# Byte distances between the matmuls' moving tiles and their weights: 64 everywhere, then 32, 48 and 80

## The chip, the cores and the metric

The kernel runs on one core of one Trainium2 chip. The metric is the device time of one execution in microseconds. Before the change it is 876.7 us, the median of 3 runs (870.92, 876.7 and 877.1 us).

## The reference

Two transformer blocks, one after the other, on 256 tokens of width 1024, all in float32. Cut to what matters:

```python
def first_block(x, p, ...):
    h = rms_norm(x, g_pre_mix); proj = h @ w_in                      # 1024 -> 1952
    o_sb = stick_breaking_attention(...); q = rms_norm(q_lat) @ w_q_up; kv = rms_norm(kv_lat) @ w_kv_up
    o_mla = mla_attention(...)
    x = x + rms_norm(concat(rms_norm(o_sb), rms_norm(o_mla)) @ w_o)
    u = causal_depthwise_conv(rms_norm(x) @ w_up)                     # 1024 -> 5632
    x = x + rms_norm((gelu(gate) * val) @ w_down)                     # 2816 -> 1024
    return x + rms_norm(sigmoid(rms_norm(x) @ w_ple_gate + b) * (p @ w_ple))

def hybrid_layer(x, mem, ...):                                        # the second block
    xn = rms_norm(x); proj = xn @ w_in                                # 1024 -> 5912
    # attention over compressed, selected and windowed keys; a 31-tap convolution; attention over mem
    merged = gates(xn) * (o_nsa @ w_nsa_out, u @ w_conv_out, o_m @ w_mem_out)
    h = x + merged @ w_out
    return h + (silu(rms_norm(h) @ w_gate) * (rms_norm(h) @ w_up)) @ w_down
```

Nearly all the work is products of a [256 x K] activation with a [K x M] weight matrix that is used once.

## The kernel before

**Weights.** All weight matrices come from memory as one stream of tiles of 128 x 1024 float32, eight blocks of 128 x 128 each. For each tile SyncE loads `raw` (a ring of 5), ScalarE rounds it into `whi` (fp32r, a ring of 6; line 1118), and VectorE or GpSimd takes the difference as `wlo` (lines 1636 and 609).

**Activations** are split the same way. Each chunk of 128 features is a row of 512 fp32r numbers in one tile: 256 high parts, then 256 low parts. `HA` holds the normed input of most stages, `ACTS` the products of both feed-forward networks, `HB` the normed memory and a few branch inputs, `HL` the latents and other small inputs.

**The product.** One 128 x 128 block of weights against one chunk takes three matmuls (`blk3`, called by `fm`), each with a weight load of its own and a moving operand of 256 columns:

```python
nc.tensor.matmul(dst, wh, hi, start=start, stop=False, skip_group_check=True)   # line 626
nc.tensor.matmul(dst, wl, hi, start=False, stop=False, skip_group_check=True)   # line 627
last = nc.tensor.matmul(dst, wh, lo, start=False, stop=stop, skip_group_check=True)   # line 628
```

In `tm` (lines 669 to 671) the roles are swapped: the activation chunk is loaded as weights, and `whi` or `wlo` moves with up to 512 columns. At lines 1010 to 1012 the loaded operand is `BS`, 30 columns (120 bytes) per step, and `whi` or `wlo` moves with 256 columns. Sums of squares (lines 683 and 688) and the attention's matmuls are plain float32.

**Addresses.** Tiles lie one behind the other in the order of their declarations, each from a multiple of 32 bytes on. The declarations around the change are

```python
SQ = sb("SQ", [P, DC, S])
sb("before_ha", [P, 112])
HA = sb("HA", [P, DC, 2 * S], F32R)
HB = sb("HB", [P, DC, 2 * S], F32R)
HL = sb("HL", [P, 4, 2 * S], F32R)
sb("behind_hl", [P, 144])
KMEM = sb("KMEM", [P, MEMH, S])
```

`raw`, `whi`, `wlo`, `X`, `Y` and `SQ` start at 0 modulo 128 bytes (in one partition). A chunk is 2048 bytes, its low half is 1024 bytes further, and a block of weights is 512 bytes, so every block and every half starts where its tile does, modulo 128. The two unused tiles move what lies behind them: 112 numbers are 448 bytes, or 64 modulo 128, and 112 + 144 = 256 numbers are 1024 bytes. The last declarations are regions that share one address, the end of everything else. Starts modulo 128, as the compiled program has them:

| tile | before | after |
|---|---|---|
| `raw`, `whi`, `wlo`, `X`, `Y`, `SQ` | 0 | 0 |
| `HA` | 64 | 32 |
| `HB` | 64 | 48 |
| `HL` | 64 | 80 |
| `KMEM`, `VMEM`, `RTT`, `RS`, `ident`, `ones`, `lower` | 0 | 96 |
| `ACTS`, `YC`, `G1`, `PX`, `QS`, `KS1`, `QM`, `KM`, `Z` | 64 | 32 |
| `BS`, step c of 16 | 64 + 120 c | 32 + 120 c |
| `VS2`, `QME`, `U`, `CY`, `PR2`, `OMEM` | 32 | 0 |

The order of all instructions on each engine is written out in the program and is not touched.

Of the kernel before, what the change touches and what calls it, by code (L numbers as in the profile page):

```python
# [9 lines left out]
F32R = mybir.dt.float32r  # L10
# [6 lines left out]
P = 128  # L17
S = 256
D = 1024
DC = D // P  # L20
# [280 lines left out]
def program(nc, stream, xT, memT, pT, pos, consts, w2, out):  # L301
    ctx = ExitStack()
    with ctx:
        def sb(name, shape, dt=F32):
            return ctx.enter_context(nc.sbuf_tensor(name, shape, dt))
# [9 lines left out]
        X = sb("X", [P, DC, S])  # L315
        Y = sb("Y", [P, DC, S])
        SQ = sb("SQ", [P, DC, S])
        sb("before_ha", [P, 112])
        HA = sb("HA", [P, DC, 2 * S], F32R)
        HB = sb("HB", [P, DC, 2 * S], F32R)  # L320
        HL = sb("HL", [P, 4, 2 * S], F32R)
        sb("behind_hl", [P, 144])
        KMEM = sb("KMEM", [P, MEMH, S])
        VMEM = sb("VMEM", [P, QT, 512])
        RTT = sb("RTT", [P, 2, 2 * S])
# [287 lines left out]
        def _(pe):  # L613
# [20 lines left out]
            def fm(stage, m, H, need=None, base=0):  # L634

                k = KC[stage]
                dst = begin((stage, m))[:, 0:S]
                for c in range(k):
                    if need is not None:
                        pe.wait_ge(a_lo, need + c + 1)  # L640
                    blk3(dst, FIRST[stage] + m * k + c, H[:, base + c, 0:S], H[:, base + c, S:2 * S],
                         c == 0, c == k - 1, c == k - 1)
# [35 lines left out]
            def stat(name, chunks, mat=ones, wide=False):  # L678

                dst = begin(("stat", name))  # L680
                if wide:
                    pe.wait_ge(sq_ready, SQ0[name] + dict(NORMS)[name])
                    nc.tensor.matmul(dst, mat[:, :], chunks, start=True, stop=True).then_inc(y_done, 1)
                    return
                for i in range(len(chunks)):
                    pe.wait_ge(sq_ready, SQ0[name] + i + 1)
                    w = 2 * CMP if name == "kc" else S
                    last = nc.tensor.matmul(dst[:, 0:w], mat[:, :], chunks[i][:, 0:w], start=i == 0,  # L688
                                            stop=i == len(chunks) - 1)
                last.then_inc(y_done, 1)  # L690
# [53 lines left out]
            def sb_pv(u):  # L744
                pe.wait_ge(sb_a, u + 1)
                o_begin(("sb", u))
                for j in range(2):
                    h = 2 * u + j
                    v = slice(h * DH, (h + 1) * DH)
                    o0 = OP[:, j * DH:(j + 1) * DH]  # L750
                    o1 = OP[:, P + j * DH:P + (j + 1) * DH]
                    nc.tensor.matmul(o0, Z[:, h, 0:P], VS1[:, 0, v], start=True, stop=True, skip_group_check=True)
                    nc.tensor.matmul(o1, Z[:, h, P:S], VS1[:, 0, v], start=True, stop=False, skip_group_check=True)
                    last = nc.tensor.matmul(o1, Z[:, h, S:384], VS1[:, 1, v], start=False, stop=True,
                                            skip_group_check=True)
                last.then_inc(o_ready, 1)
# [75 lines left out]
            def turn_out(use, src, ready, count):  # L832

                pe.wait_ge(ready, count)
                t_begin(use)
                for c in range(4):
                    for qt in range(QT):
                        last = nc.tensor.transpose(TP[:, c * S + qt * P:c * S + (qt + 1) * P],
                                                   src[:, qt, c * P:(c + 1) * P], ident[:, :])
                    if c == 1:  # L840
                        last.then_inc(t_half, 1)
                last.then_inc(t_ready, 1)
# [24 lines left out]
            for name, m in UPS:  # L867
                if name == "qup":
                    fm("qup", m, HL, SP0["ql"] if m == 0 else None)
                    if m == 0:  # L870
                        sb_cum(3)
                else:
                    if m == 1:
                        wait_freed(pe, ("sbv", 1))
                    if m:
                        sb_pv(m - 1)
                    fm("kup", m, HL, SP0["kvl"] if m == 0 else None, base=2)
            sb_pv(3)
# [16 lines left out]
            scores(("mla", 1))  # L895
            tm("vup", 512, HL, base=2)
            fm("memk", 0, HB, SP0["mem"])
            turn_out(("osb", 0), OSB, o_normed, 2)
# [20 lines left out]
            for m in range(1, 4):  # L919
                fm("memk", m, HB)  # L920

# [31 lines left out]
            for m in range(2):  # L953
                fm("ple", m, HL, SP0["p"] if m == 0 else None)
            stat("postffn", [SQ[:, c, :] for c in range(8)])
            for m in range(2, 8):
                fm("ple", m, HL)
            stat("plegate", [SQ[:, c, :] for c in range(8)])
# [3 lines left out]

            tm("memv", 512, HB, ks=range(0, 5))
            stat("mix2", [SQ[:, c, :] for c in range(8)])
            tm("memv", 512, HB, ks=range(5, 8))

# [54 lines left out]
            def fill(item, between=None):  # L1021
# [33 lines left out]
                if name in ("gnsb", "brnsa"):  # L1055
                    fm(name, m, HA if name == "gnsb" else HL, SP0["on"] if name == "brnsa" and m == 0 else None)
                    return
                H, base, split = {"brmem": (HB, 4, "om"), "brconv": (HB, 0, "cv")}[name]
                b = FIRST[name] + 12 * m
# [33 lines left out]
            for m in range(8):  # L1093
                fm("wout", m, HB, SP0["y"] if m == 0 else None)

# [1355 lines left out]
```

## Time and profile before

| | |
|---|---|
| median of 3 runs | 876.7 us |
| the profiled execution | 873.64 us |
| its span, first to last instruction | 871.9 us |
| TensorE busy | 826.1 us (95%), 6722 matmuls in the records |
| weight loads busy | 789.6 us (91%) |
| VectorE, ScalarE, GpSimd busy | 638.7, 498.8, 317.6 us |
| mean granted TensorE clock | 0.994 |

Matmuls overlap: the record of one lasts longer than the distance from its start to the next one's start. What a stream of matmuls costs is therefore read from the starts in the timeline (the last start less the first, divided by the intervals between them), and not from the mean duration. The other runs have times but no traces.

### The profile page before, as it was taken

How to read it: one execution, taken by the hardware profiler on the slowest of the kernel's cores; microseconds unless marked ns; L12 is line 12 of the kernel's file. 1: busy time of each engine (PE TensorE's matmuls, PEld its weight loads, DVE VectorE, ACT ScalarE, POOL GpSimd, SP SyncE). 2: the span in 40 equal slices, each digit the busy share in tenths (PEclk: the TensorE clock that was granted, in tenths of full speed). 3: DMA queues.
4: the chain of work that ended last, by engine and by line, in shares of the span. 5: the costliest groups of instructions: out<-in, count | busy, mean ns of one | idle time of the engine just before them, and what ended most of it. 6: DMA issues, size and time to landing. Idle time of an engine off the chain costs nothing.

```text
span 871.9 us, 16984 instructions
## 1 busy us (share of the span) xinstructions
PE 826.1 (95%) x6722; PEld 789.6 (91%) x6722; DVE 638.7 (73%) x981; ACT 498.8 (57%) x914; POOL 317.6 (36%) x148
## 2 busy tenths in 40 slices
PE   4999999999999999999999789899999999999998
PEld 3998889899999999788999779788999999999998
DVE  6895764888887772768799889955665676667774
ACT  6665655854665657756766474367546544444441
POOL 3843213122333225344466534332454223322321
PEclk9999999999999999999999999999999999999999
DMA  5743234355766665352656542322464457666651
GB/s 209 269 157 107 73 98 145 99 181 152 242 222 188 199 192 170 111 172 98 202 171 192 178 137 74 96 73 77 142 190 149 146 171 230 183 193 191 194 170 49
DMA packets 57246, 137.18 MB, mean 157 GB/s; under 512 B 6352, under 2 KB 27088, under 8 KB 57168
## 3 DMA queue, kind: packets, MB, share of 16 engines
q1 hardware_dynamic: 57168, 136.11, 49.4%
q8 instruction: 53, 0.87, 0.4%
q14 instruction: 25, 0.20, 0.1%
HBM read 135.03 MB, written 1.05 MB: 156 GB/s over the span
## 4 chain that ended last, share of the span: by engine, by line
PE 78%; DVE 10%; ACT 6%; issue 4%; DMA 1%; SPq 0%; DVEq 0%; ACTq 0%
PE PROD L626 15%; PE PROD L627 15%; PE PROD L628 15%; PE PROD L688 3%; PE OP L626 2%; PE OP L627 2%; PE OP L628 2%; PE SC L627 2%; PE TP L627 2%; PE TP L628 2%; PE SC L628 2%; PE TP L626 2%; PE SC L626 2%; DVE RS L1644 2%; PE OP L828 2%
## 5 line engine op out<-in xcount | busy, mean ns | idle before, releaser
L609 POOL TENSOR_TENSOR wlo<-raw,whi 128x1024 fp32r<-128x1024 f32 x124 | 314.0, 2538 | 533.8 <-ACT whi L1118 509.0
L626 PE MATMUL PROD<-HA,whi 128*128 128x256 f32 x1088 | 308.0, 283 | 13.1 <-DVE HA L1665 6.4
L627 PE MATMUL PROD<-HA,wlo 128*128 128x256 f32 x1088 | 302.9, 278 | 0.0
L628 PE MATMUL PROD<-HA,whi 128*128 128x256 f32 x1088 | 302.7, 278 | 0.0
L1118 ACT ACTIVATE whi<-raw 128x1024 fp32r<-128x1024 f32 x252 | 262.7, 1055 | 57.7 <-PE PROD L628 31.5
L1636 DVE TENSOR_TENSOR wlo<-raw,whi 128x1024 fp32r<-128x1024 f32 x128 | 191.0, 1495 | 82.4 <-ACT whi L1118 82.2
L626 PEld LDWEIGHTS PROD<-HA,whi 128*128 128x128 f32 x1088 | 205.9, 189 | 16.5 <-DVE HA L1665 7.0
L627 PEld LDWEIGHTS PROD<-HA,wlo 128*128 128x128 f32 x1088 | 205.3, 189 | 0.8 <-issue 0.7
L628 PEld LDWEIGHTS PROD<-HA,whi 128*128 128x128 f32 x1088 | 205.2, 189 | 0.0
L1644 DVE RECIPROCAL RS<-RTT 128x256 f32<-128x256 f32 (+2 forms) x18 | 42.8, 2380 | 16.6 <-ACT RTT L1137 16.5
L626 PE MATMUL OP<-HA,whi 128*128 128x256 f32 x192 | 53.7, 280 | 0.7 <-DVE KS L1721 0.5
L628 PE MATMUL OP<-HA,whi 128*128 128x256 f32 x192 | 53.1, 276 | 0.0
L627 PE MATMUL OP<-HA,wlo 128*128 128x256 f32 x192 | 53.1, 276 | 0.0
L688 PE MATMUL PROD<-SQ,ones 128*128 128x256 f32 x144 | 37.5, 403 | 12.3 <-ACT SQ L1130 12.2
L626 PE MATMUL SC<-ACTS,whi 128*128 128x256 f32 x176 | 48.6, 276 | 0.0
L627 PE MATMUL SC<-ACTS,wlo 128*128 128x256 f32 x176 | 48.6, 276 | 0.0
L628 PE MATMUL SC<-ACTS,whi 128*128 128x256 f32 x176 | 48.6, 276 | 0.0
L626 PE MATMUL TP<-ACTS,whi 128*128 128x256 f32 x176 | 48.6, 276 | 0.0
L627 PE MATMUL TP<-ACTS,wlo 128*128 128x256 f32 x176 | 48.6, 276 | 0.0
L628 PE MATMUL TP<-ACTS,whi 128*128 128x256 f32 x176 | 48.6, 276 | 0.0
L626 PE MATMUL PROD<-HB,whi 128*128 128x256 f32 x160 | 46.4, 290 | 0.0
L627 PE MATMUL PROD<-HB,wlo 128*128 128x256 f32 x160 | 45.3, 283 | 0.0
(330 smaller groups left out, 1622.0 us busy)
## 6 DMA issues: line engine op xcount, KB each, us to landing
raw<-stream SPq DMA_DIRECT2D x197, 512.0 KB, 4.1
raw<-stream SPq DMA_DIRECT2D x144, 128.0 KB, 2.6
raw<-stream SPq DMA_DIRECT2D x28, 256.0 KB, 3.0
raw<-stream SPq DMA_DIRECT2D x4, 384.0 KB, 3.2
X<-xT SPq DMA_DIRECT2D x2, 512.0 KB, 5.5
out<-X SPq DMA_DIRECT2D x8, 128.0 KB, 2.0
KMEM<-memT SPq DMA_DIRECT2D x1, 512.0 KB, 5.4
VMEM<-memT SPq DMA_DIRECT2D x1, 512.0 KB, 6.1
```

What stands on the lines that cost most here:

```text
L609: nc.gpsimd.tensor_tensor(wlo[:, n % NSPLIT, :], raw[:, n % NRAW, :], whi[:, n % NSPLIT, :].bitcast(F32), ALU.subtract).then_inc(lo_pool, 1)
L626: nc.tensor.matmul(dst, wh, hi, start=start, stop=False, skip_group_check=True)
L627: nc.tensor.matmul(dst, wl, hi, start=False, stop=False, skip_group_check=True)
L628: last = nc.tensor.matmul(dst, wh, lo, start=False, stop=stop, skip_group_check=True)
L688: last = nc.tensor.matmul(dst[:, 0:w], mat[:, :], chunks[i][:, 0:w], start=i == 0, stop=i == len(chunks) - 1)
L828: last = nc.tensor.matmul(OP[:, j * dv:(j + 1) * dv], PT[0:w, i * P:(i + 1) * P], v, start=kb == 0, stop=kb == nkb - 1, skip_group_check=True)
L1118: nc.scalar.activation(whi[:, n % NSPLIT, :], raw[:, n % NRAW, :], ACT.Copy).then_inc(hi_done, 1)
L1636: nc.vector.tensor_tensor(wlo[:, n % NSPLIT, :], raw[:, n % NRAW, :], whi[:, n % NSPLIT, :].bitcast(F32), ALU.subtract).then_inc(lo_vector, 1)
L1644: nc.vector.reciprocal(dst[:, 0:width], RTT[:, RT[name] % 2, 0:width]).then_inc(rs_ready, 1)
```

## The change

It sizes the two unused tiles anew and gives `HB` and `HL` 8 numbers more than they hold, of which the tile used is the middle part, 16 bytes further on. Nothing else is edited: both programs issue the same instructions in the same order on TensorE, VectorE, ScalarE, GpSimd and SyncE, and only addresses differ.

```diff
         SQ = sb("SQ", [P, DC, S])
-        sb("before_ha", [P, 112])
+        sb("before_ha", [P, 104])
         HA = sb("HA", [P, DC, 2 * S], F32R)
-        HB = sb("HB", [P, DC, 2 * S], F32R)
-        HL = sb("HL", [P, 4, 2 * S], F32R)
-        sb("behind_hl", [P, 144])
+        HB = sb("HB", [P, 2 * DC * S + 8], F32R)[:, 4:2 * DC * S + 4].rearrange("p (c s) -> p c s", c=DC)
+        HL = sb("HL", [P, 8 * S + 8], F32R)[:, 4:8 * S + 4].rearrange("p (c s) -> p c s", c=4)
+        sb("behind_hl", [P, 128])
         KMEM = sb("KMEM", [P, MEMH, S])
```

## Rows read from the trace of the kernel before

**Rows 1.** Busy tenths of TensorE, weight loads and granted clock, 40 slices of the span.
```profile
PE   4999999999999999999999789899999999999998
PEld 3998889899999999788999779788999999999998
PEclk9999999999999999999999999999999999999999
```

**Rows 2.** Matmuls by shape: columns, then busy us, mean ns, idle before.
```profile
L626 PE MATMUL PROD<-HA,whi 128*128 128x256 f32 x1088 | 308.0, 283 | 13.1 <-DVE HA L1665 6.4 <-DVE HA L1895 2.3 <-ACT CW L1491 1.7
L626 PE MATMUL OP<-HA,whi 128*128 128x256 f32 x192 | 53.7, 280 | 0.7 <-DVE KS L1721 0.5 <-DVE HA L1665 0.2
L626 PE MATMUL SC<-ACTS,whi 128*128 128x256 f32 x176 | 48.6, 276 | 0.0
L626 PE MATMUL TP<-ACTS,whi 128*128 128x256 f32 x176 | 48.6, 276 | 0.0
L626 PE MATMUL PROD<-HB,whi 128*128 128x256 f32 x160 | 46.4, 290 | 0.0
L688 PE MATMUL PROD<-SQ,ones 128*128 128x256 f32 x142 | 37.2, 406 | 12.3 <-ACT SQ L1130 12.2
L626 PE MATMUL PROD<-HL,whi 128*128 128x256 f32 x68 | 19.9, 293 | 2.4 <-DVE HB L2268 2.4
```

**Rows 3.** Timeline of TensorE, 300 to 320 us: start us, us; first and last of 179 matmuls.
```profile
299.81 0.28 PE L626 MATMUL PROD<-HA,whi 128*128 128x256 f32 x1
...
319.98 0.28 PE L627 MATMUL PROD<-HA,wlo 128*128 128x256 f32 x1
```

**Rows 4.** Timeline of TensorE, 360 to 380 us: the 2nd and the last of 173 matmuls.
```profile
359.86 0.28 PE L627 MATMUL PROD<-HA,wlo 128*128 128x256 f32 x1
...
380.00 0.28 PE L627 MATMUL PROD<-HA,wlo 128*128 128x256 f32 x1
```

**Rows 5.** TensorE by stretch, the two feed-forward networks: length, busy (matmuls), clock, DMA share, GB/s.
```profile
169.90:344.60 174.70, 174.70 (x1544) 1.00 0.63 195
690.00:871.90 181.90, 178.40 (x1572) 1.00 0.55 170
```

**Rows 6.** The same view, three of the eleven longest stretches outside them.
```profile
360.00:382.20 22.20, 22.20 (x191) 1.00 0.57 173
440.00:456.60 16.60, 16.60 (x142) 1.00 0.59 196
663.60:683.70 20.10, 20.10 (x173) 1.00 0.57 178
```

**Rows 7.** Timeline of TensorE at the start of the first feed-forward network.
```profile
169.34 0.28 PE L627 MATMUL PROD<-HA,wlo 128*128 128x256 f32 x1
169.46 0.28 PE L628 MATMUL PROD<-HA,whi 128*128 128x256 f32 x1
169.57 0.28 PE L626 MATMUL PROD<-HA,whi 128*128 128x256 f32 x1
169.70 0.28 PE L627 MATMUL PROD<-HA,wlo 128*128 128x256 f32 x1
169.82 0.28 PE L628 MATMUL PROD<-HA,whi 128*128 128x256 f32 x1
169.93 0.28 PE L626 MATMUL PROD<-HA,whi 128*128 128x256 f32 x1
```

**Rows 8.** Timeline of TensorE, `BS` loaded (30 columns): first and last of 24 matmuls.
```profile
475.20 0.28 PE L1012 MATMUL PROD<-whi,BS 128*30 128x256 f32 x1
...
477.89 0.28 PE L1011 MATMUL PROD<-wlo,BS 128*30 128x256 f32 x1
```

**Rows 9.** The same matmuls 11 us later: first and last of 8.
```profile
486.59 0.42 PE L1010 MATMUL PROD<-whi,BS 128*30 128x256 f32 x1
...
488.08 0.42 PE L1011 MATMUL PROD<-wlo,BS 128*30 128x256 f32 x1
```

**Rows 10.** That stretch: length, busy of PE, PEld, DVE, ACT, POOL, then clock, DMA.
```profile
485.90:489.10 3.20, 3.15 (x15) 2.58 (x16) 3.20 (x1) 0.00 (x0) 0.00 (x0) 0.50 0.68 189
```

**Rows 11.** Timeline: 16 plain float32 matmuls; then `HB` loaded, first and last of 29.
```profile
382.36 3.61 PE L688 MATMUL PROD<-SQ,ones 128*128 128x256 f32 x16
...
387.28 0.39 PE L670 MATMUL PROD<-wlo,HB 128*128 128x512 f32 x1
...
393.69 0.40 PE L671 MATMUL PROD<-whi,HB 128*128 128x512 f32 x1
```

**Rows 12.** Waits, longest in total: us in total, times, longest.
```profile
ACT whi L1118 <- PE PROD L628: 31.5, 34, 2.0
DVE RS L1644 <- ACT RTT L1137: 16.5, 6, 3.2
PE PROD L688 <- ACT SQ L1130: 12.2, 6, 6.9
ACT whi L1118 <- DMA raw<-stream: 9.8, 5, 2.8
```

**Rows 13.** The chain that ended last, shares of the span by engine.
```profile
PE 78%; DVE 10%; ACT 6%; issue 4%; DMA 1%; SPq 0%; DVEq 0%; ACTq 0%
```

## The prediction

> **What bounds the kernel now.** I read the shares by slice first: TensorE is busy in nine tenths or more of nearly every slice, and over each of the two feed-forward networks it is never idle, while the DMA engines are busy for 0.63 and 0.55 of the time [rows 1, 5]. The chain that ended last runs through TensorE for 78% [rows 13]. Of the waits, the longest of TensorE's own comes to 12.2 us in all, and ScalarE waits 31.5 us for TensorE to free a weight buffer against 9.8 us for a tile to land [rows 12]. So the stream of matmuls sets the time, and the weights are ready ahead of it. The change moves no instruction. The only thing that it can alter is how long one instruction takes, and the only kind numerous enough to matter is the fp32r matmul of 256 columns whose moving operand is a chunk of `HA`, `ACTS`, `HB` or `HL`: 1088 + 192 + 176 + 176 + 160 + 68 = 1860 blocks [rows 2], three matmuls each, **5580 matmuls**. 1632 of the 1860 blocks, 88%, move `HA` or `ACTS`, the tiles that go from 64 to 32.
>
> **What such a matmul costs now.** The starts in the timeline tell. From 299.81 to 319.98 us there are 178 intervals, 20.17 / 178 = **113.3 ns** each [rows 3]. From 359.86 to 380.00 us there are 171, 20.14 / 171 = **117.8 ns** [rows 4]. Both stretches have the full clock [rows 1], the same tile `HA`, the same weights' rings, the same distance of 64 bytes. So one distance knows two paces. Each holds without a break until something interrupts the stream: the first network goes through 1544 matmuls at 113.3 ns [rows 5], the stretches at 117.8 ns are up to 191 long [rows 6]. The pace is settled in the first few matmuls after a pause. At the start of the first network three intervals of about 0.12 us come, one of 0.13, one of 0.12, and from there on the stream is at 0.11 [rows 7]. Stepping through all starts of the 5580, 3841 intervals are of 113 or 114 ns, 1568 of 117 to 121 ns, and the other 170 hold a wait or a change of pace; of the 1568, 1077 lie in eleven stretches like those of [rows 6], the rest in pieces of 10 to 50 between the attention's matmuls. Put together: at 113.3 ns throughout, this execution would be 1568 x (117.8 - 113.3) ns = **7.0 us** shorter; at 117.8 ns throughout, 3841 x 4.5 ns = **17.3 us** longer.
>
> **Is anything below 113.3 ns in sight?** At the low clock (0.50) the same 256 columns take 1.49 / 7 = 213 ns [rows 9, 10], and half of that would be 106.5 ns: at the high clock 6.8 ns are lost per matmul that are not lost at the low one. Plain float32 matmuls, which take the array at half the pace, show 16 in 3.61 us, (3.61 - 0.41) / 15 = 213 to 215 ns for 256 columns, or 107 ns for half of it [rows 2, 11]: nothing lost there either, and their moving tile lies at distance 0 from `ones`. With 512 moving columns the interval is 6.41 / 28 = 229 ns against 213 ns [rows 11]: the loss is some 16 ns, twice or more that of 256 columns, though the weight load is the same 128 columns. So the larger part of the loss goes with the moving columns and not with the load. And the one place where distances vary is `BS`: each of the 16 steps loads it from another address modulo 128, eight bytes from the last. Its 23 intervals take 2.69 / 23 = 117.0 ns on the mean [rows 8], no single one below 113 ns in the timeline. This speaks for a floor of 113.3 ns that no distance undercuts, and for a second loss of up to 4.5 ns that depends on how load and moving stream meet. It is weak: `BS` is 30 columns of load, not 128, and changes every third matmul.
>
> **The change part by part.**
> - `HA` and `ACTS` from 64 to 32 (1632 x 3 = 4896 matmuls). No row shows a steady stream at 32. Bounds from rows: below, 107 ns (nothing lost); above, 113.3 + 6.7 = 120 ns (the moving operand starts off a multiple of 64 bytes, so its 1024 bytes touch 17 pieces of 64 instead of 16, and one piece is 16 columns, 1/16 of 107 ns). I take neither end but the mix of the two paces that stand in [rows 3, 4], the nearest rows: same tile, same shape. Cost 0, between -7.0 and +17.3 us with the lock, -33 and +29 us at the ends.
> - `HB` to 48 and `HL` to 80: 228 x 3 = 684 matmuls, at 117.8 ns for 448 of them already (345 and 103 by the timeline). All of them at either pace moves -2.0 to +0.8 us. Cost 0.
> - Swapped roles (`tm`, distance 64 to 96, 48 or 80): about 160 matmuls, the widest at 229 ns per 512 columns; 3 to 5 ns each either way is under 1 us.
> - `ones`, `ident` and `lower` to 96 against `SQ` and `Y` at 0: 142 matmuls of the shape in [rows 2] and some hundred of other shapes, at half the pace, with nothing lost now. At most the 4.5 ns of above each, about +1 us.
> - Vector, scalar and DMA operands shifted by 16 or 32 bytes: no row shows a dependence, and what they work on is ahead of TensorE by the waits named above. Cover, if gone: none of it is nearer than the weights' path, which leaves 37% of the DMA engines' time in the networks [rows 5]. Cost 0.
>
> The sum against the profiled execution is 0: 873.6 us. That execution had both networks at the fast pace. The first one at the slow pace would cost 1544 x 4.5 ns = 6.9 us, which is about the spread of the three runs (870.9 to 877.1); I take it, as an estimate, that executions differ in which pace a network catches. The profiled one is 3.1 us under the median of 876.7, so I forecast between them: **875 us**, own range 868 to 885.
>
> The Trainium skill ("TensorE: Matmul & The Clock Gate", "Step-by-step: what each phase is for") says that TensorE has two independent read ports into SBUF, so that loading the next weights takes no bandwidth from the running matmul. By it the distance is without a price, the sum is exactly 0 and the split of paces has some other cause. The trace sides with it on the larger part of the loss, which grows with moving columns, and leaves open the 4.5 ns; that is why "no change" leads but with less than half.
>
> **The rivals.**
> - **The new distance always finds the fast pace** (20%). For it: after a pause the stream often changes from the slow to the fast pace [rows 7] and the reverse never shows inside a stretch. Against it: 191 matmuls in a row without the change at the same distance [rows 6]. Time: 873.6 - 7.0 = 866.6, 867 us, 1.1% under the median.
> - **The floor itself falls** (7%). If the 6.7 ns come from the meeting of load and stream, and 32 avoids it, all 5580 go to 107 ns: 5580 x 6.3 ns = 35 us and the 7.0, 832 us. Against it the 512 columns and `BS`, above. The Trainium skill (same page, "Back-to-back issue gap") gives 262 cycles for 256 columns, 109.2 ns at 2.4 GHz. By that figure the estimate for this rival is 843 us. No fp32r row of this trace comes near it.
> - **The slow side: the new distance always locks at 117.8 ns** (20%). The place is the two networks, 3116 matmuls that now run at 113.3 ns and could be caught for their whole length by a pace that nothing interrupts. It decides from the first dozen matmuls after 169 and 690 us. Price 17.3 us with the rest: 891 us, 1.6% over the median. For it: nearly two thirds of what lies outside the networks (1568 of 5580 - 3116 = 2464) is at this pace today, so it is as easy to catch.
> - **Off the 64-byte multiple costs a piece** (11%). All moving operands of fp32r start at 0 or 64 now, after the change at 32, 48 or 80. 3841 x 6.7 ns + 1568 x 2.2 ns = 29 us: 903 us. Nothing in the trace moves an fp32r operand from such an address, so nothing excludes it. The Trainium skill ("SBUF — State Buffer", "Specifications (TRN2)") gives lines of 16 bytes; by that rule 32, 48 and 80 touch no more lines than 64, and this rival would cost nothing.
> - That the change does not do what it says is not a rival: the compiled addresses are 32, 48 and 80 modulo 128.
>
> **How the numbers follow.** 42% for the forecast, 20, 7, 20 and 11% for the rivals. A measurement of this kernel tells about 1% from no change (its runs spread by 0.7%), which is 868 to 885 us. Faster by more: 20 + 7 = 27%; within: 42%; slower by more: 20 + 11 = 31%. The range takes the forecast, the fast lock and the slow lock, 82%, with 3 to 5 us for the small terms: 862 to 893 us.
>
> **What would show it.** In the timeline of the changed kernel, the intervals from start to start inside the two networks: 113.3 ns is the forecast or the first rival, which the stretch from 360 us on tells apart (117.8 or 113.3 ns); 117.8 ns in the networks is the third; near 120 the fourth; under 113 the second, and my floor is wrong. The 512-column matmuls at 229 ns and the plain float32 ones at 215 ns should stay. If the paces are as before and the time is not, then a wait has changed that I have put at nothing, and the place to look is ScalarE's rounding and the landing of `raw`. The prediction is wrong at its root if the new distances bring a pace that no row here has.

## The result, and the profile after

The changed kernel takes **890.8 us**, the median of 4 runs (889.05 to 891.83), against 876.9 us for the kernel before on the same chip (4 runs, 870.92 to 878.2). The ratio is 1.0147 [1.0103, 1.0191]: slower, by more than the 1% that the prediction took as the least that can be told. Ratios here and below are formed from the undisturbed executions alone, so they need not equal the quotient of the medians. The profiled execution takes 891.83 us, its span is 890.1 us. The time lies inside the range of 862 to 893 us; the forecast, no change at 875 us, was wrong.

The page first: busy engines, then the shares of the chain that ended last.

```profile
PE 848.4 (95%) x6722; PEld 812.7 (91%) x6722; DVE 630.4 (71%) x981; ACT 500.6 (56%) x914; POOL 318.3 (36%) x148
PE 83%; DVE 7%; ACT 5%; issue 4%; DMA 1%; SPq 0%; DVEq 0%; ACTq 0%
```

The chain runs through TensorE for 83% instead of 78% [rows 13], with the same 6722 matmuls. The groups by shape (busy us and mean ns of one behind the bar, then idle time before them):

```profile
L626 PE MATMUL PROD<-HA,whi 128*128 128x256 f32 x1088 | 312.8, 288 | 12.8 <-DVE HA L1665 6.4 <-DVE wlo L1636 2.6 <-DVE HA L1895 2.2
L626 PE MATMUL SC<-ACTS,whi 128*128 128x256 f32 x176 | 49.4, 281 | 0.0
L626 PE MATMUL PROD<-HB,whi 128*128 128x256 f32 x160 | 46.0, 288 | 0.0
L688 PE MATMUL PROD<-SQ,ones 128*128 128x256 f32 x142 | 37.7, 409 | 11.8 <-ACT SQ L1130 11.7
```

Each matmul on `HA` and `ACTS` has grown by 5 ns (283 to 288, 276 to 281), those on `HB` have not (290 to 288) [rows 2], and the idle time in front of them is what it was. But this column is the length of one record, which overlaps the next ones, so it can hide a change of 5 ns in the pace: the starts show that `HB` has slowed as well, from 116.8 to 119.2 ns. The timeline of TensorE, twice: from 299.76 to 319.94 us, the first ten and the last of 171 matmuls in a row, and from 371.81 to 389.99 us, the first and the last of 156.

```profile
299.76 0.28 PE L628 MATMUL PROD<-HA,whi 128*128 128x256 f32 x1
299.88 0.28 PE L626 MATMUL PROD<-HA,whi 128*128 128x256 f32 x1
300.00 0.28 PE L627 MATMUL PROD<-HA,wlo 128*128 128x256 f32 x1
300.12 0.28 PE L628 MATMUL PROD<-HA,whi 128*128 128x256 f32 x1
300.24 0.28 PE L626 MATMUL PROD<-HA,whi 128*128 128x256 f32 x1
300.36 0.28 PE L627 MATMUL PROD<-HA,wlo 128*128 128x256 f32 x1
300.48 0.28 PE L628 MATMUL PROD<-HA,whi 128*128 128x256 f32 x1
300.60 0.28 PE L626 MATMUL PROD<-HA,whi 128*128 128x256 f32 x1
300.72 0.28 PE L627 MATMUL PROD<-HA,wlo 128*128 128x256 f32 x1
300.83 0.28 PE L628 MATMUL PROD<-HA,whi 128*128 128x256 f32 x1
...
319.94 0.28 PE L627 MATMUL OP<-HA,wlo 128*128 128x256 f32 x1
...
371.81 0.28 PE L628 MATMUL PROD<-HA,whi 128*128 128x256 f32 x1
...
389.99 0.28 PE L627 MATMUL PROD<-HA,wlo 128*128 128x256 f32 x1
```

20.18 / 170 = **118.7 ns** in the network, where it was 113.3 [rows 3], and 18.18 / 155 = **117.3 ns** in the stage outside it, where it was 117.8 [rows 4]. The first of these paces does not occur before. Close up, the pattern repeats every five intervals: 116 or 117, 119, 122, 120 and 116 ns (the rows, in hundredths of a us, show them as 0.12 and 0.11). Of the 3726 intervals on `HA` without a wait 8 are of 114 ns or less, of 1055 on `ACTS` none.

Both traces hold the same 6722 matmuls in the same order, so they can be compared at the same matmul. Starts in us:

| from, to | before | after | difference |
|---|---|---|---|
| start, first matmul on `ACTS` in network 1 | 185.6 | 188.5 | +2.9 |
| the next 1391 intervals (network 1) | 157.6 | 165.1 | +7.5 |
| from there to the first on `ACTS` in network 2 | 367.5 | 368.0 | +0.5 |
| the next 1391 intervals (network 2) | 157.6 | 165.1 | +7.5 |
| last matmul to the end of the span | 3.5 | 3.5 | 0 |

So 15.0 of the 18.2 us come from the two networks, 5.4 ns for each of 2782 intervals. The small net difference outside them hides a larger one. Over all 5417 intervals of the main matmuls (fp32r, 256 columns, moving `HA`, `ACTS`, `HB` or `HL`) that have full clock and no wait in both traces (none is above 130 ns), the sum is 21.1 us, of which 6.3 us lie outside the two networks' stretches. The intervals that touch the lower clock in either trace add 0.8 us (the mean granted clock is 0.990 instead of 0.994), and all others, most of them with a wait, give back about 3.6 us. The medians differ by 4 us less than the profiles (13.9 us) because the profiled execution of before is one of its faster ones, and that of after the slowest of its four. TensorE is never idle in a stretch inside the first network, before and after; full clock, and a lower share of the DMA engines because the same weights are spread over more time (length, busy, clock, DMA share, GB/s; the second stretch is of network 2):

```profile
175.00:353.00 178.00, 178.00 (x1502) 1.00 0.58 184
705.00:890.10 185.10, 181.84 (x1533) 1.00 0.52 163
```

ScalarE waits longer for TensorE to give a weight buffer back, 47.5 us where it was 31.5 [rows 12]: a slower TensorE, not a cause.

```profile
ACT whi L1118 <- PE PROD L628: 47.5, 48, 2.3
```

The rest is as it was: plain float32 matmuls on `SQ` still start every 215 ns, the 512-column ones take 231.7 ns on the mean (229.8 before).

### The profile page after: what moved, and what is told of

It is laid out like the page before. It is cut to its first block, busy times and chain, and to the rows that moved or that the text cites. A ratio compares the mean times of both kernels' runs of the same rounds, so it can differ in the third digit from the quotient of the medians.

```text
span 890.1 us, 16984 instructions
## 1 busy us (share of the span) xinstructions
PE 848.4 (95%) x6722; PEld 812.7 (91%) x6722; DVE 630.4 (71%) x981; ACT 500.6 (56%) x914; POOL 318.3 (36%) x148
## 4 chain that ended last, share of the span: by engine, by line
PE 83%; DVE 7%; ACT 5%; issue 4%; DMA 1%; SPq 0%; DVEq 0%; ACTq 0%
PE PROD L626 16%; PE PROD L628 16%; PE PROD L627 16%; PE PROD L688 3%; PE OP L626 3%; PE OP L628 2%; PE OP L627 2%; PE SC L627 2%; PE TP L627 2%; PE TP L626 2%; PE SC L626 2%; PE TP L628 2%; PE SC L628 2%; PE OP L828 2%; ACT whi L1118 2%
## 5 line engine op out<-in xcount | busy, mean ns | idle before, releaser
L626 PE MATMUL PROD<-HA,whi 128*128 128x256 f32 x1088 | 312.8, 288 | 12.8 <-DVE HA L1665 6.4
L1118 ACT ACTIVATE whi<-raw 128x1024 fp32r<-128x1024 f32 x252 | 263.4, 1055 | 82.7 <-PE PROD L628 47.5
L628 PE MATMUL PROD<-HA,whi 128*128 128x256 f32 x1088 | 307.8, 283 | 0.0
L627 PE MATMUL PROD<-HA,wlo 128*128 128x256 f32 x1088 | 307.7, 283 | 0.0
L1636 DVE TENSOR_TENSOR wlo<-raw,whi 128x1024 fp32r<-128x1024 f32 x128 | 186.4, 1458 | 84.8 <-ACT whi L1118 84.8
L627 PEld LDWEIGHTS PROD<-HA,wlo 128*128 128x128 f32 x1088 | 207.9, 191 | 0.8 <-issue 0.7
L688 PEld LDWEIGHTS PROD<-SQ,ones 128*128 128x128 f32 x144 | 27.3, 202 | 19.8 <-issue 9.5
```

The source lines that it names most:

```text
L1118: nc.scalar.activation(whi[:, n % NSPLIT, :], raw[:, n % NRAW, :], ACT.Copy).then_inc(hi_done, 1)
L1636: nc.vector.tensor_tensor(wlo[:, n % NSPLIT, :], raw[:, n % NRAW, :], whi[:, n % NSPLIT, :].bitcast(F32), ALU.subtract).then_inc(lo_vector, 1)
```

## The experiments

Three theories at the start, named as in the expectations. **D**: the distance between what is loaded and what moves sets a pace of its own for each value; the address itself does not matter. **A**: an address off a multiple of 64 bytes costs, distance or not. **N**: the pace comes from what other engines do to the memory at the same time. Two came later. **S**: a distance that looks fast is only a lucky start. **P**: the period is 256 or 512 bytes, not 128. "Pace" is the mean interval from start to start at full clock; distances are from the start of the loaded to that of the moving operand, in bytes.

### p1_distances: streams of matmuls alone

In place of the two blocks stand streams of matmuls: 36 fp32r matmuls of 256 columns each, `whi` and `wlo` loaded in turn as `blk3` does it, no other engine at work meanwhile, 16 distances, six different starts each (plain matmuls ahead and the length of a pause).

```diff
+PLAN += [(0, d, 128, 256, lead, pause, 36) for d in range(0, 128, 8)
+         for lead, pause in ((0, 16), (0, 137), (0, 401), (2, 16), (3, 90), (1, 300))]
```

> Only streams of fp32r matmuls (128 columns loaded, 256 moving), the blocks of the reference are left out: 16 distances from 0 to 120 in steps of 8 bytes, weights at 0 modulo 128, each six times for 36 matmuls after a pause. Theory D (the distance decides which repeating patterns of intervals exist, the start after a pause which of them is caught): at 64 streams settle at 113.3 or 117.8 ns, at 32 at 117.3 or 118.7 ns, never at 113.3; the others fall between 113 and 121 ns, and the six starts of one distance give at most two or three values. Theory A (a moving operand off a multiple of 64 bytes costs a piece): 0 and 64 at 113.3 to 117.8 ns, all fourteen others near 118 to 120 ns. Theory N (other engines' accesses set the pace, not the distance): all sixteen the same, since no other engine works here.

Measured, in ns: 0 118.9; 8 120.0; 16 **113.3** from all six starts; 24 120; 32 118.9; 40 120; 48 118.4; 56 120.8; 64 113.3 (one start of seven 118.9); 72 120.5; 80 118.4; 88 120.5; 96 121.1; 104 120.3; 112 118.2; 120 121.4. Theory N falls: the paces are there with TensorE alone. A falls in its simple form: 0 is slow and 16 fast. What I did not see at this point: in this program `wlo` lay 128 bytes further modulo 256 than in the kernel. It matters below.

### p2_offsets: distance or address

```diff
+PLAN += [(w, d, 128, 256, lead, pause, 36) for w, d in
+         ((32, 64), (96, 64), (32, 32), (64, 32), (96, 32), (64, 96), (16, 64), (4, 64), (0, 60), (0, 68))
+         for lead, pause in LEADS]
+PLAN += [(0, d, 30, 256, lead, pause, 36) for d in (0, 32, 64) for lead, pause in LEADS]
```

(and the same distances with 512 and with 128 moving columns; `w` is the weights' own offset.)

> Only streams of fp32r matmuls, the blocks of the reference are left out. Weights at 32, 96, 64, 16 or 4 modulo 128 with distances 64, 32 and 96; then 30 columns loaded; then 512 and 128 columns moving. Theory D: the address of the weights itself is without effect, so weights at 32, 96, 16 and 4 with distance 64 settle at 113.3 or 117.8 ns, and weights at 32 and 96 with distance 32 at 117.3 or 118.7 ns, though weights at 32 with distance 32 have the moving operand at 64. Theory A: weights at 32 with distance 64 (moving at 96) near 118 to 120 ns; weights at 32 with distance 32 (moving at 64) at 113.3 ns. With 30 columns loaded theory D expects less dependence on the distance, and all near 113 to 117 ns; with 512 columns moving 226.7 ns (17/16 of 213.3) at 64 and some 231 ns at 32; with 128 columns moving no theory has a firm number, since the load of 128 columns may bound it.

Distance 64 gives the two paces 113.3 and 118.9 with the weights at 0, at 32 and at 96; distance 32 gives 118.9 with the weights at 32, 64 and 96. A moving operand at 96 reaches 113.3, one at 64 with distance 32 does not. So A falls altogether, and with it the prediction's piece of 64 bytes. Below multiples of 32 the weights' own address does count (distance 64 with weights at 16: 118.3, at 4: 120.6). With 30 columns loaded, distance 32 settles at 113.3 from all starts, 0 at 113.3 from five of six (the sixth stays at 120.0), and 64 runs at 115.5 to 116.7. With 512 moving, 0 runs at 231.3, 32 at 233.2 and 64 at 233.1 with one start at 228.8, not in the order that was expected. With 128 moving, all three distances run at 111.7. So the dependence is there in every shape tried but the one with 128 moving columns.

### e1_ha32: only HA and ACTS moved

```diff
-        sb("before_ha", [P, 112])
+        sb("before_ha", [P, 104])
         HA = sb("HA", [P, DC, 2 * S], F32R)
+        sb("before_hb", [P, 8])
...
+        sb("before_acts", [P, 24])
```

> The kernel before with HA and ACTS (and the tiles that share the region) at 32 modulo 128; HB and HL stay at 64, ones, ident, lower, KMEM at 0. Theory D: this is 88% of the matmuls concerned and both networks, so nearly all of the loss: 1.2 to 1.5% slower than before, 887 to 890 us, intervals of 117.3 to 118.7 ns in the networks. If instead the loss came from HB, HL or the plain float32 matmuls against ones, it stays at 877 us.

891.03 us (888.89 to 893.61), ratio 1.0187 [1.014, 1.0234]. The timeline of TensorE, first and last of 171:

```profile
299.81 0.28 PE L630 MATMUL PROD<-HA,whi 128*128 128x256 f32 x1
...
319.90 0.28 PE L629 MATMUL OP<-HA,wlo 128*128 128x256 f32 x1
```

20.09 / 170 = 118.2 ns. `HA` and `ACTS`, with the tiles that share the address of `ACTS`, give the whole loss. `HB` and `HL`, put back, run at 114.6, and that is not seen in the time.

### e2_all_by_32: everything moved together

```diff
+        sb("before_raw", [P, 8])
         raw = sb("raw", [P, NRAW, TILE])
```

> The kernel before with one unused tile of 32 bytes ahead of all others: weights at 32, HA, HB, HL and ACTS at 96, so every distance stays 64 while every address leaves its multiple of 64. Theory D: no change, 870 to 878 us, intervals of 113.3 and 117.8 ns. Theory A: slower by the extra piece, 890 to 903 us.

878.22 us (869.5 to 881.6), ratio 1.0044 [1.001, 1.0078]; both networks of the profiled execution take 157.6 us as before. First and last of 179:

```profile
299.78 0.28 PE L628 MATMUL PROD<-HA,wlo 128*128 128x256 f32 x1
...
319.95 0.28 PE L629 MATMUL PROD<-HA,whi 128*128 128x256 f32 x1
```

20.17 / 178 = 113.3 ns, as [rows 3]. With every tile 32 bytes off, and the distances kept, the pace stays. The interval of the ratio does lie just above 1: 9 of the 12 executions take 878 to 882 us and three 869.5 to 872.3, where of before beside it 4 of 17 take 876.7 to 880.7 and 13 take 869.8 to 872.9. Why more of them are in the upper group is open. A asked for at least 890 us, so this still settles D against A in the whole kernel.

### p3_around_16: how narrow the fast distance is

```diff
+PLAN += [(w, d, 128, 256, lead, pause, 48) for w, d in
+         ((0, 4), (0, 12), (0, 20), (0, 16), (16, 16), (32, 16), (48, 16), (64, 16), (80, 16), (96, 16), (112, 16))
+         for lead, pause in LEADS]
```

> Only streams of fp32r matmuls, the blocks of the reference are left out. Distances 4, 12, 20 and 16 with weights at 0, then distance 16 with weights at 16 to 112; then 30 columns loaded; then 512 moving at distances 16, 48, 80, 96, 112. Theory D (distance alone): distance 16 settles at 113.3 ns from every start and for weights at 0, 32, 64 and 96; 4, 12 and 20 at 118 to 121 ns like 8 and 24 in the first scan. Theory S (16 is a lucky start, as 64 can be): some of the starts, or some of the weights' offsets, settle near 118 ns. Weights at 16, 48, 80 and 112 are open: weights at 16 with distance 64 stood at 118.3 ns, so they may be slower. 30 columns loaded at 16: 113.3 ns. 512 columns moving: between 227 and 234 ns, no theory orders them.

Distance 16 runs at 113.3 from all starts with the weights at 0, 32, 64 and 96, and at 117.8 to 118.6 with them at 16, 48, 80 and 112, but for one start of the 24, which stays at 115.6 (at 112). Distances 4, 12 and 20 take 122.4, 117.8 and 120 to 121. Two more rows of this run: 30 loaded columns at distance 16 take 115.7 ns, not the 113.3 that was expected, and at 96 about 117; 512 moving columns take 228.7 to 233.3 at five distances. So the fast case is a point, not a region, and needs the weights on a multiple of 32.

### e3_all_at_16: a miss

```diff
-        sb("before_ha", [P, 112])
-        HA = sb("HA", [P, DC, 2 * S], F32R)
...
+        def moved(name, chunks, at):
+            return sb(name, [P, chunks * 2 * S + 32], F32R)[:, at:at + chunks * 2 * S].rearrange(
+                "p (c s) -> p c s", c=chunks)
+
+        HA = moved("HA", DC, 4)
+        HB = moved("HB", DC, 4)
+        HL = moved("HL", 4, 4)
...
+        ACTS = ACTS[:, 20:20 + FC * 2 * S].rearrange("p (c s) -> p c s", c=FC)
```

> The kernel before with HA, HB, HL and ACTS at 16 modulo 128 and the weights at 0; other tiles as before. Theory D with the scan's 113.3 ns at distance 16 from each of six starts: every stage settles at 113.3 ns within a dozen matmuls, so this run loses the 1568 slow intervals of before, 866 to 868 us where before has its fast networks at 871 to 873 us, and its runs do not split into two clusters: ratio to before 0.990 to 0.996. Theory S (the scan's 16 is luck): as before, 870 to 880 us, in two clusters.

890.17 us (888.15 to 891.77), ratio 1.0172 [1.0118, 1.0227]: as slow as the change. `ACTS` runs at 117.9, `HA` at 113.3 only in places (862 of 3742 intervals). First and last of 171, 20.12 / 170 = 118.4 ns:

```profile
299.77 0.28 PE L630 MATMUL OP<-HA,whi 128*128 128x256 f32 x1
...
319.89 0.28 PE L632 MATMUL PROD<-HA,whi 128*128 128x256 f32 x1
```

The distance modulo 128 is 16 here as in the streams, and the pace is another. So 128 is not the period. Laying the addresses side by side showed it: in the kernel `whi` and `wlo` agree modulo 512, in the streams they lay 128 bytes apart modulo 256, and the tiles of this kernel are at 16 (`HA`, `HL`) and 144 (`HB`, `ACTS`) modulo 256.

### e4_all_at_0: how much the distance of before is worth

The edit is that of the last kernel with `moved(..., 0)` and `ACTS` from 16 on, so that every distance is 0 modulo 128.

> The kernel before with HA, HB, HL and ACTS at 0 modulo 128, the distance that tiles have if nobody moves them. Theory D with the scan's 118.9 ns: some 5400 matmuls at 118.9 ns, against before 3841 x 5.6 + 1568 x 1.1 = 23 us more, 893 to 897 us. If the scan does not carry over to the kernel, it stays between 870 and 880 us.

896.12 us (894.94 to 898.9), ratio 1.0241 [1.0178, 1.0305]; first and last of 170, 20.22 / 169 = 119.6 ns, each network 166.2 us:

```profile
299.77 0.28 PE L631 MATMUL PROD<-HA,wlo 128*128 128x256 f32 x1
...
319.99 0.28 PE L632 MATMUL OP<-HA,whi 128*128 128x256 f32 x1
```

So the placement of before is worth some 20 us against one with all four tiles at 0. That is not the same as leaving out the two unused tiles, though the expectation says so: together they are 1024 bytes, so without them `ACTS` would still be at 64, and here it was moved by an edit of its own. No run leaves out just the two.

### e5_hb48_hl80: only HB and HL moved

```diff
-        HB = sb("HB", [P, DC, 2 * S], F32R)
-        HL = sb("HL", [P, 4, 2 * S], F32R)
-        sb("behind_hl", [P, 144])
+        HB = sb("HB", [P, 2 * DC * S + 28], F32R)[:, 28:].rearrange("p (c s) -> p c s", c=DC)
+        HL = sb("HL", [P, 8 * S + 8], F32R)[:, 4:8 * S + 4].rearrange("p (c s) -> p c s", c=4)
+        sb("behind_hl", [P, 8])
```

> The kernel before with only HB at 48 and HL at 80; HA and ACTS stay at 64, ones and the rest at 0. 684 matmuls, 448 of them at 117.8 ns before; the scan has 118.4 ns for both distances: +1 us at most. 871 to 879 us, no change that can be measured. If these tiles carried a part of the loss of the whole change, 2 us or more.

877.48 us (874.46 to 884.41), ratio 1.003 [0.9991, 1.0069]: nothing to be told, as expected. It brought something that I had not meant: `ACTS` slid from 192 to 64 modulo 256 (both 64 modulo 128), and of its 1055 intervals none is at 113.3, all are at 117.8, while `HA`, still at 192, keeps its pace (networks 160.0 us each). The same distance modulo 128, two behaviours. It also means that this run does not isolate `HB` and `HL`: `ACTS` costs it 2.4 us in each network (160.0 against 157.6), inside the same result.

### p4_mod_512: the period

```diff
+PLAN += [(0, d, 128, 256, lead, pause, 42) for d in range(0, 512, 16)
+         for lead, pause in ((0, 16), (2, 16), (3, 90), (1, 300))]
```

with `whi` and `wlo` both at 0 modulo 512, as in the kernel.

> Only streams of fp32r matmuls, the blocks of the reference are left out. In the first two scans whi and wlo were 128 bytes apart modulo 256, which they are not in the kernel; here both are at 0 modulo 512, as in the kernel to each other, and the distance goes from 0 to 496 in steps of 16. In the kernels so far, ACTS at distance 192 modulo 512 (before) settled at 113.3 ns, at 64 or 320 (the fifth experiment) at 117.8, at 160 (the change) at 118.7, at 144 (the third) at 117.8, HA at 272 in places at 113.3. Theory P (the period is 256 or 512 bytes, not 128): the scan gives different paces for 64 and 192 and for 16 and 144, and repeats the kernels' numbers. Theory D as first stated (only the distance modulo 128 counts): 16, 144, 272 and 400 all alike, and so 64, 192, 320, 448.

Everything repeats after 256 bytes. From 0 on in steps of 16, ns: 120.0, 116.7, 116.7, 118.3, 117.8, 120.0, 120.0, **113.3**, 118.8, 118.7, 118.6, 119.3, **117.8 or 113.3**, 119.2, 118.3, 117.1. Rows of its timeline, each pair from one stream, at distance 112 (27 intervals), at 160 (39), and twice at 192 (39 each, from two starts):

```profile
194.38 0.28 PE L372 MATMUL PS<-H,wlo 128*128 128x256 f32 x1
...
197.44 0.28 PE L372 MATMUL PS<-H,wlo 128*128 128x256 f32 x1
...
263.87 0.28 PE L372 MATMUL PS<-H,wlo 128*128 128x256 f32 x1
...
268.49 0.28 PE L372 MATMUL PS<-H,wlo 128*128 128x256 f32 x1
...
311.69 0.28 PE L372 MATMUL PS<-H,wlo 128*128 128x256 f32 x1
...
316.28 0.28 PE L372 MATMUL PS<-H,wlo 128*128 128x256 f32 x1
...
323.85 0.28 PE L372 MATMUL PS<-H,wlo 128*128 128x256 f32 x1
...
328.27 0.28 PE L372 MATMUL PS<-H,wlo 128*128 128x256 f32 x1
```

3.06 / 27 = 113.3; 4.62 / 39 = 118.5; 4.59 / 39 = 117.7; 4.42 / 39 = 113.3 ns. The last two are one distance that keeps either of two paces, that of the kernel before. Put beside the kernels (means of their intervals at full clock):

| distance mod 256 | in the streams | in the kernels |
|---|---|---|
| 0 | 120.0 | 119.9 (`HA`, e4) |
| 16 | 116.7, one start 118.6 | 113.3 in places, else slower (`HA`, e3) |
| 32 | 116.7, one start 117.8 | 116.9 (`ACTS`, e1) |
| 48 | 118.3 | 118.3 (`HB`, e5) |
| 64 | 117.8 | 117.8 (`ACTS`, e5) |
| 80 | 120.0 | 119.0 (`HL`, e5) |
| 128 | 118.8 | 118.7 (`ACTS`, e4) |
| 144 | 118.7 | 117.9 (`ACTS`, e3) |
| 160 | 118.6 | 118.4 (`HA`), 118.7 (`ACTS`), after |
| 176 | 119.3 | 119.2 (`HB`), after |
| 192 | 113.3 or 117.8 | 113.3 and 117.8, before |
| 208 | 119.2 | 119.0 (`HL`), after |

The streams' column is for both weights' tiles in step; in the kernels' column one tile stands for each distance. Nine of twelve are within 0.3 ns. The three that miss (16, 80, 144) miss by about 1 ns or by a second pace.

### e6_scan_layout, p5_two_distances, e7_all_at_112, e8_192_and_64: can it be won?

The layout of the first streams, with `wlo` 128 bytes further, copied with all its remainders (e6):

```diff
+        sb("before_wlo", [P, 32])
...
+        sb("before_ha", [P, 96])
+        H = sb("H", [P, 20 * 2 * S + 4], F32R)[:, 4:20 * 2 * S + 4].rearrange("p (c s) -> p c s", c=20)
+        HA, HB, HL = H[:, 0:8], H[:, 8:16], H[:, 16:20]
+        sb("behind_hl", [P, 24])
...
+        ACTS = ACTS[:, 116:116 + FC * 2 * S].rearrange("p (c s) -> p c s", c=FC)
```

> The kernel before with the layout of the scan's stream that reached 113.3 ns from all starts: wlo 128 bytes further on modulo 256, so that HA, HB, HL and ACTS are at 272 from whi and 144 from wlo, modulo 512. Theory P: the layout carries over with all its residues, 113.3 ns everywhere, 865 to 868 us and no second cluster. If what makes the pace in the kernel is more than addresses (other engines' accesses), 872 to 892 us.

Every longer stretch now runs at 113.3 after at most 15 matmuls; first and last of 179, 20.17 / 178:

```profile
299.74 0.28 PE L629 MATMUL PROD<-H,whi 128*128 128x256 f32 x1
...
319.91 0.28 PE L627 MATMUL PROD<-H,whi 128*128 128x256 f32 x1
```

And yet 873.75 us (869.96 to 876.71) against 874.17, ratio 0.9986 [0.9955, 1.0017]. Then all pairs of both distances, in search of a pace below 113.3 or one that is reached sooner:

```diff
+PLAN += [(0, d, shift, 256, lead, pause, 24) for shift in range(0, 256, 32) for d in range(0, 256, 16)
+         for lead, pause in ((0, 16), (2, 16), (1, 300))]
```

> Only streams of fp32r matmuls, the blocks of the reference are left out. whi's distance from 0 to 240 in steps of 16, and wlo shifted against whi by 0 to 224 in steps of 32, each after three different starts, 24 matmuls. Theory P (the residues of both distances modulo 256 decide the pace): the row of shift 0 repeats the last scan, 113.3 ns at 112 alone from every start and at 192 from some; shift 128 repeats the first scan, 113.3 ns at 16. Others open; no stream below 113.3 ns. If a stream falls below 113.3 ns, the floor is a matter of addresses too.

None of the 128 pairs goes below 113.3 ns, and the slowest takes 124. From all three starts only three reach it: `wlo` in step with distance 112, and `wlo` 128 further with 16 or 192. Two of these in the kernel, e7 (distance 112) and e8 (192, with `wlo` at 64):

```diff
-        sb("before_ha", [P, 112])
+        sb("before_ha", [P, 88])
+        H = sb("H", [P, 20 * 2 * S + 4], F32R)[:, 4:20 * 2 * S + 4].rearrange("p (c s) -> p c s", c=20)
...
+        ACTS = ACTS[:, 12:12 + FC * 2 * S].rearrange("p (c s) -> p c s", c=FC)
```

> The kernel before with HA, HB, HL and ACTS at 112 modulo 256 from whi and wlo. Theory P: 113.3 ns in every stretch after 3 to 14 matmuls, as in the scan; the networks' 3116 matmuls at 113.3 ns as in the fast runs of before, and the stretches outside them faster. The sixth experiment, with another such layout, gained 3 to 4 us on the profiled span of before and nothing on the median; here the same, 868 to 875 us. Theory D (modulo 128 alone): 112 had 118.2 ns in the first scan, so 888 to 893 us.

```diff
+        sb("before_wlo", [P, 32])
...
-        sb("before_ha", [P, 112])
+        sb("before_ha", [P, 80])
+        H = sb("H", [P, 20, 2 * S], F32R)
...
-        sb("behind_hl", [P, 144])
+        sb("behind_hl", [P, 16])
```

> The kernel before with HA, HB, HL and ACTS at 192 modulo 256 from whi, as they are, and wlo 128 bytes further on, so at 64 from it: of the 128 pairs of distances in the fifth scan the one that reached 113.3 ns soonest on the mean of three starts (0.03 us lost over 22 matmuls, 0.04 to 0.05 us for the next). Theory P: 113.3 ns in every stretch, the two networks' stretch of 1391 intervals at 157.6 us each as in the fast runs of before, no runs with a network at the slow pace. Median 868 to 873 us against 870 to 877 of before. If what is won outside the networks is given back by waits and by the clock, as in the sixth and seventh experiments, 872 to 876 us and no difference that can be measured.

e7: 875.85 us (874.53 to 880.95), ratio 1.0041 [1.0015, 1.0068], if anything slower. e8: 873.58 us (871.18 to 875.11), ratio 0.9997 [0.9968, 1.0026]. The matmuls did get faster. Taken at the same matmuls as in the trace of before, and only where both have full clock and no wait, the intervals of the main ones sum to 4.4 us less in e6, 4.6 us less in e7 and 5.1 us less in e8. But the spans are 873.1 us in e7 and 871.8 in e8 against 871.9; that of e6, its fastest execution, is 868.2, and its median is not lower either, though 865 to 868 us were expected. The networks take 157.6 us in all of them, so the saving was outside them, and there the traces give it back: in e8 the intervals that touch the lower clock in either trace are 4.9 us longer; in e7 these are 3.6 us longer and all the rest 2.2 us. In the same two stretches (length, TensorE's busy time, clock, DMA share), first the kernel before:

```profile
125.00:135.00 10.00, 7.89 (x62) 1.00 0.19 59
500.00:510.00 10.00, 7.63 (x62) 1.00 0.50 168
```

then e8, and e7 in the first of the two:

```profile
125.00:135.00 10.00, 7.98 (x51) 0.83 0.21 59
500.00:510.00 10.00, 8.09 (x56) 0.83 0.48 157
```

```profile
125.00:135.00 10.00, 7.89 (x51) 0.83 0.19 56
```

A mean of 0.83 is a third of the stretch at the lower level, 1.2 instead of 2.4 GHz. Over the whole span e8 spends 23.8 us at that level, before 10.7 us. It would be easy to call this the price of the faster matmuls, and it is not shown. The kernel of e1, whose matmuls are slower than before's, has the same dip in the first stretch and 20.4 us at the lower level in all, and the changed kernel, slower as well, dips in the second and has 18.2 us in all:

```profile
125.00:135.00 10.00, 8.62 (x57) 0.83 0.17 57
```

```profile
500.00:510.00 10.00, 8.05 (x47) 0.83 0.73 262
```

So the one trace of before is one with little time at the lower level. The mean granted clock of every execution gives the time at that level for all of them (twice the missing share, times the span): on the mean 19.3 us in e6 against 18.8 in the runs of before beside it, 23.5 against 16.4 in e7, 21.8 against 19.2 in e8. At half speed the differences cost at most 0.3, 3.6 and 1.3 us. The clock can account for much of what e7 did not gain, and for little in e6 and e8. What e8 did bring is a narrower spread: none of its 12 runs is above 875.2 us, while 4 of 17 runs of before beside it lie at 877.8 to 880.7. But e7, whose streams reach the fast pace from every start too, has 5 of 12 at 878.3 to 881.0.

## Why the prediction was wrong, step by step

- **The step that failed** is the first of the change part by part: "I take neither end but the mix of the two paces that stand in [rows 3, 4], the nearest rows: same tile, same shape. Cost 0". Same tile and same shape, but not the same distance, and the distance is what sets the pace (p2, e2). At the new one neither row applies: a third pace of 118.7 ns takes the place of 113.3 in both networks, 15 of 18.2 us. Put into the prediction's own sum, 3841 intervals x 5.4 ns = 20.7 us, and 0 to 1 ns for each of the other 1568; the traces show 21.1 us more in the main matmuls, where the prediction had 0. The text itself had the sentence for it, "wrong at its root if the new distances bring a pace that no row here has", and gave it no chance of its own.
- **The sum against the median.** 873.6 + 18.2 = 891.8 us for the profiled execution of after. The chances of a slower kernel (31%) were too low: the present distance reaches 113.3 for two thirds of its intervals, and with the floor that the prediction itself argued for there are 7.0 us to win and 17.3 to 29 us to lose. The bounds of 107 and 120 ns held: 118.7 lies within them, near the upper one. (A slip without weight: 873.6 less 35 and 7.0 is 831, not 832.)
- **The third rival had the number, not the reason.** "Always locks at 117.8", 891 us, is 0.2 us from the measured median. But the pace is 118.7, with a pattern of its own, and it is not caught at the start of a network: it is all that this distance knows outside a few intervals (8 of 3726 are fast).
- **The fourth rival** (an address off a multiple of 64 costs a piece, 903 us) is refuted by e2 and p2. The Trainium skill ("SBUF — State Buffer", "Specifications (TRN2)"), with its lines of 16 bytes, was on the right side about this piece. But e1 shows that this does not make such a move free.
- **The second rival and the floor.** No distance goes below 113.3 ns, in 16 distances, 32 and 128 pairs. The floor argued from `BS` and the 512 columns held: streams with 30 loaded columns take 113.3 to 117 ns by distance, with one start at 120.0, and never less (p2, p3). The Trainium skill ("TensorE: Matmul & The Clock Gate", "Back-to-back issue gap") gives 262 cycles for 256 columns of a matmul by itself, 109.2 ns at 2.4 GHz; no fp32r stream of 256 columns here comes to it.
- **The two read ports.** The distance alone changes the pace from 113.3 to 120.0 ns with no other engine at work (p4), which loading beside a running matmul should not do by the rule of two independent read ports that the prediction took from the Trainium skill (the same page, "Step-by-step: what each phase is for"). With 512 moving columns the paces span 228.7 to 233.3 ns, with 128 there is no difference at three distances (111.7). Here the measurement decides, and it speaks against the sum of exactly 0. What the load and the moving operand share is not shown by it.
- **What held.** `HB` and `HL` are worth nothing that can be measured (e1 has the whole loss without them), though for another reason than I gave: they go to 119 ns, but most of them were at the slow pace, and 684 x 2.4 ns = 1.6 us at most. Plain float32 stayed, and 512 columns moved by 2 ns in 93 intervals. Nothing outside TensorE became slower by more than 2 us (VectorE busy for 630.4 us instead of 638.7, ScalarE 500.6 instead of 498.8, GpSimd 318.3 instead of 317.6).
- **The estimate that executions of before differ in which pace a network catches** is open. Only one execution of before has a trace. For it: its 17 runs beside e1 fall into two groups some 7 us apart, near the 6.9 us worked out, those beside e8 into two some 8 us apart, those beside e3 to e5 into three (869.5 to 872.6, 876.2 to 879.6 and 882.7 to 886.8 us), as none, one or both networks at the slow pace might give, and e8 itself has one group. Against it: e7, with 113.3 ns from every start in the streams, has two groups, some 4 us apart.

What stays open: what in the hardware meets when two operands are 112 or 192 bytes apart modulo 256 and not otherwise; and where the 4 to 5 us that the matmuls of e6 and e8 gained have gone, beyond what the clock explains.

## What to carry to other kernels

Where a kernel is bound by fp32r matmuls with a weight load each, put the relative placement of loaded and moving tiles on the list of what to tune, and measure it with short streams of matmuls alone that copy every remainder modulo 256 of the real tiles, both weights' tiles among them, and several starts: one such run told nine of twelve placements to 0.3 ns, and a copy modulo 128 gave a miss. Read the pace from starts, not from durations, and do not carry a pace from one distance to another because tile and shape are the same. A change that costs 5 ns per matmul in the bound stages is paid nearly in full (21.1 us in the matmuls, 18.2 us in the span); one that saves 5 ns in stages that also wait can come to nothing (e6 to e8).

## What the runs showed of the hardware that I had not expected

- The pace of an fp32r matmul (128 columns loaded, 256 moving) depends on the distance between the two operands modulo 256 bytes: 113.3 ns at 112, 113.3 or 117.8 at 192, 116.7 to 120.0 elsewhere, where both weights' tiles are in step (p4). With one of them shifted against the other the pattern is another, 113.3 to 124 ns over 128 pairs (p5). The common address does not matter to the pace in multiples of 32 bytes (p2, e2).
- It is bistable at some distances: at 192 in the streams (p4) 113.3 and 117.8 ns each hold to the end, and the start picks one. In `HA` before, 191 matmuls stay slow and 1544 fast; changes from slow to fast occur inside a stretch.
- 113.3 ns is the lowest of all, 17/16 of the 106.7 ns that 256 columns would take at one per cycle of 2.4 GHz. At the lower clock the same columns take 213 ns [rows 9], nothing lost.
- Weights at 16 modulo 32 lose the fast pace of distance 16 (117.8 to 118.6 against 113.3, one start 115.6; p3), and distances off a multiple of 16 were never fast (117.8 to 122.4; p1 to p3).
- The time at the lower clock differs between executions of one program: of 17 executions of before beside e8 the mean granted clock is 0.986 to 0.994, some 24 to 10 us of the span.
